# Four weight chunks of the fourth expert moved out of the ring, in a transformer block with 32 experts

## The chip, the cores and the metric

The kernel runs on one core of a Trainium2 chip. The metric is the device time of one execution in microseconds; the time before is the median of three runs. The profile is that of one execution. Its span runs from the first to the last instruction; its own device time, a little longer, stands beside it in the table below.

## The reference, cut to what matters

One layer over 512 tokens of width 2048, all in float32: a combined projection, sliding-window attention and trailing mean pools, an output projection, cross attention to 256 memory tokens, and then a mixture of experts:

```python
h = rmsnorm(x, ffn_norm_g)
g_sel  = argmax(h @ rg_w + rg_b)                    # one of 4 groups
top_v, top_i = top_k(e_logits of that group, 2)     # 2 of its 8 experts
y = (silu(xb @ w_gate[e]) * (xb @ w_up[e])) @ w_down[e]   # d_ff 512
x = x + sum over the 2 picks of gate * y
```

Each of the 32 experts has three float32 matrices of 2048 x 512 or 512 x 2048, 12 MiB together; all 32 are read, 384 MiB.

## The kernel before, in words

Front stages (attention, pools, output projection, cross attention) fill the first 700 us. The router follows: `turn_router` and `logits` on TensorE give the logits, a chain of small VectorE operations (L1299 to L1388) makes the tables of which token sits in which of the 64 slots of which expert, and GpSimd gathers the rows of the first two experts from `hn_dram`, a copy of the normed rows in device memory (`gather`, L588). Semaphore `logits_done` comes with the last logits, `table_ready` with the last table (L1388).

Then 32 expert blocks run, one for each expert, two to a pair. `block_pe(b, par, pair)` multiplies 64 slots with gate and up (L1893, 64 matmuls, chunks 0 to 7), then with down (L1921, 32 matmuls, chunks 8 to 11). In an even block it also adds the pair before to the tokens (`spread_parts`, L1870 with `y_hi` and L1871 with `y_lo`, the upper and lower half of the split rows; VectorE writes `y_lo` at L1423 and adds at L1405). At the end of the gate and up part of an odd block, `turn_rows` (L1850) turns the rows of the next pair, which the gather brought. Blocks 0 and 1 stand written out, blocks 2 to 31 are a loop over pairs.

The weights come through a ring of 12 buffers (`slot(s)`), one chunk of 1 MiB each, one expert in all. All weight loads are issued in order by SyncE (SP). `load_expert(e, b)` waits, before it loads chunk j, until TensorE has finished with chunk j of the block before (`used` counts finished chunks), and `landed[s]` tells TensorE of the arrival. The 12 chunks of expert 0 are issued while cross attention ends (L438), those of the others as blocks free their buffers (L444). `expert_slot(j)` gives the buffer of chunk j.

Buffers of SBUF are reused by hand. `Hf` is the buffer of transposed activations, of which the expert blocks use the first 3072 columns of 8192, and columns 4096 to 6143 under the name `y_lo` (tensor `below_y_low` is only there to place it). `PB` is the buffer of the projection: `hs[:, 0]` and `hs[:, 1]` are its first 4096 columns, the router's tables lie in 4096 to 8191, and the ramp of tokens in 6656 to 7167. `kx` and `vx` hold memory keys and values until cross attention ends; the router's padded logits `L` use part of `vx`.

Of the kernel before, what the change touches and what calls it, by code (L numbers as in the profile page):

```python
# [12 lines left out]
P = 128  # L13
F32 = mybir.dt.float32
I32 = mybir.dt.int32
F32R = mybir.dt.float32r
# [21 lines left out]
NE = NG * EPG  # L38
FF = 512
# [4 lines left out]
SLOTS = 64  # L44
# [8 lines left out]
POOL_BANKS = (4, 6, 7)  # L53
SCORE_BANKS = (0, 2, 1, 3)
NSLOT = 12
NA = 4
NCOL = NG + NE


def hybrid_block(nc, x, mem, mix_norm_g, w_in, q_norm_g, k_norm_g, sink_logits, pool_w, pool_scale,  # L60
# [5 lines left out]
    with ExitStack() as ctx:  # L66
        def sb(name, shape, dt=F32):
            return ctx.enter_context(nc.sbuf_tensor(name, shape, dt))

        def sem(name):  # L70
            return ctx.enter_context(nc.semaphore(name))
# [17 lines left out]
        X = sb("residual", [P, NT, D])  # L89
        with nc.sbuf_tensor("mix_high", [P, KD, S], F32R) as mix_hi:  # L90
            pass
        with ExitStack() as shared:
            shared.enter_context(nc.sbuf_tensor("below_y_low", [P, 4096], F32))
            y_lo = shared.enter_context(nc.sbuf_tensor("y_low", [P, 4, 512], F32R))
        H = sb("transposed_acts", [P, KD, S])
        with ExitStack() as shared:
            shared.enter_context(nc.sbuf_tensor("below_y", [P, 2 * D], F32))
# [4 lines left out]
        PB = sb("proj_buffer", [P, NCT * S])  # L102
        with ExitStack() as shared:
            tri_r = shared.enter_context(nc.sbuf_tensor("lower_triangle", [P, P], F32R))
            ones_r = shared.enter_context(nc.sbuf_tensor("ones_rounded", [P, P], F32R))
            M_r = shared.enter_context(nc.sbuf_tensor("picks_of_token", [P, NT + 1, NE], F32R))
            P_r = shared.enter_context(nc.sbuf_tensor("slot_of_pick", [P, 2 * NT, SLOTS], F32R))
            shared.enter_context(nc.sbuf_tensor("below_block_tokens", [P, 96], F32))
            Bv_r = shared.enter_context(nc.sbuf_tensor("block_tokens", [P, 2 * NT, TCOL], F32R))
        kx = sb("memory_keys_T", [P, XH, NM])  # L110
        vx = sb("memory_values", [P, NM // P, XW])
        ident = sb("identity", [P, P])
# [18 lines left out]
        def slot(s):  # L131
            return ring[:, s * CHK:(s + 1) * CHK]
# [20 lines left out]
        Hf = H[:, :, :].rearrange("p k s -> p (k s)")  # L153
        PTX = slot(7)[:, 0:1024]
        qn = slot(7)[:, 1024:1536].rearrange("p (h n) -> p h n", n=XD)
        junk = slot(7)[:, 1536:2048]
        xsT = Hf[:, 0:KD * P].rearrange("p (k n) -> p k n", n=P)
        act_t = Hf[:, 2048:2048 + KF * SLOTS]
        sil = Hf[:, 2304:2304 + KF * SLOTS]
        gu = Hf[:, 2560:2560 + FF]  # L160
# [27 lines left out]

        landed = [sem(f"landed{s}") for s in range(NSLOT)]
        used = sem("chunks_used")  # L190
        mem_in = [sem("mem_in0"), sem("mem_in1")]
        x_in = [sem(f"x_in{t}") for t in range(NT)]
        gain_in = sem("gain_in")
# [205 lines left out]
        def expert_chunk(e, j):  # L399

            if j < 8:
                return (gate_v, up_v)[j % 2][ds(e, 1), :, j // 2, :].rearrange("e p m -> p (e m)")
            return down_v[ds(e, 1), :, j - 8, :].rearrange("e p n -> p (e n)")


        def expert_slot(j):
            return (4, 5, 6, 0, 1, 2, 3, 7, 8, 9, 10, 11)[j]

        @block.sync
        def _(sp):  # L410
            for t in range(2):
                sp.dma_start(memx[:, t, :], mem[0, t * P:(t + 1) * P, :]).then_inc(mem_in[t], 16)
            for n, (s, src, width) in enumerate(early):
                if n in (2, 3):
                    for t in range(2 * n - 4, 2 * n - 2):
                        sp.dma_start(X[:, t, :], x[0, t * P:(t + 1) * P, :]).then_inc(x_in[t], 16)
                if n == SEQ_OUT + 1:
                    sp.wait_ge(halves_used, HALVES_IN)
                if n == SEQ_OUT + 3:
                    for t in range(NT):  # L420
                        sp.dma_start(X[:, t, :], x[0, t * P:(t + 1) * P, :]).then_inc(x_again, 16)
                if n == SEQ_XO:

                    sp.wait_ge(halves_used, HALVES_IN + 32)
                last = [m for m in range(n) if early[m][0] == s]
                if last:
                    sp.wait_ge(used, last[-1] + 1)
                sp.dma_start(slot(s).rearrange("p (k n) -> p k n", n=width), src).then_inc(landed[s], 16)
            for j in range(12):
                s = expert_slot(j)  # L430
                if 3 <= j < 6:
                    sp.wait_ge(used, SEQ_XQ + s + 1)
                if j == 6:
                    sp.wait_ge(xq_done, NT)
                if j == 7:
                    sp.wait_ge(o_done, 28)
                    sp.wait_ge(parts_done, 32)
                sp.dma_start(slot(s), expert_chunk(0, j)).then_inc(landed[s], 16)  # L438

            def load_expert(e, b):  # L440
                for j in range(12):
                    s = expert_slot(j)
                    sp.wait_ge(used, b * 12 + (UE - 12 + j + 1))
                    sp.dma_start(slot(s), expert_chunk(e, j)).then_inc(landed[s], 16)  # L444

            with sp.Fori(1, NE) as b:
                load_expert(b, b)
            sp.wait_ge(table_ready, 1)
            more = sp.value_load(meta[0:1, NOVER:NOVER + 1], min_val=0, max_val=NOVER)
            with sp.If(more > 0):  # L450
                with sp.Fori(0, NOVER) as j:
                    e = sp.value_load(meta[0:1, ds(j, 1)], min_val=0, max_val=NE - 1)
                    load_expert(e, j + NE)
            for t in range(NT):
                sp.wait_ge(sum_ready, 2 * t + 2)
                sp.dma_start(out[0, t * P:(t + 1) * P, :], X[:, t, :]).then_inc(stored, 16)
            sp.wait_ge(stored, 16 * NT)
# [993 lines left out]
        def _(pe):  # L1451
# [401 lines left out]

            def expert_landed(b, j):
                s = expert_slot(j)
                pe.wait_ge(landed[s], b * 16 + 16 * (early_loads[s] + 1))

            def spread_parts(before, half, last=False):

# [20 lines left out]
            def block_pe(b, par, pair):  # L1880
                if par == 0:
                    pe.wait_ge(xsT_ready, b * 2 + 4)
                wait_past(pe, gu_copied, b)
                for c in range(4):
                    for kk in range(4):
                        k = 4 * c + kk
                        for side in range(2):

                            j = 2 * c + side
                            if kk == 0:  # L1890
                                expert_landed(b, j)
                            w = slot(expert_slot(j)).rearrange("p (k n) -> p k n", n=FF)
                            ins = mm(ps[side * SLOTS:(side + 1) * SLOTS, 0, :], xsT[:, k, par * SLOTS:(par + 1) * SLOTS], w[:, kk, :],  # L1893
                                     start=(k == 0), stop=(k == KD - 1), skip_group_check=True)
                            if kk == 3:
                                ins.then_inc(used, 1)
                if par == 1:
                    if pair is not None:
                        pe.wait_ge(part_added, pair * 8)
                    turn_rows(1 if pair is None else pair + 1)  # L1900
                behind = par == 0 and pair is not None
                if behind:

                    pe.wait_ge(y_dve, b * 2)
                    pe.wait_ge(spread_ready, pair)
                    spread_parts(pair * 8 - 8, 0)
                pe.wait_ge(gu_copied, b + 1)
                for f in range(KF):
                    ins = turn(guT[:, f, :], gu[:, f * P:(f + 1) * P], ident[:, :])
                ins.then_inc(gu_turned, 1)  # L1910
                if behind:
                    spread_parts(pair * 8 - 8, 1)
                pe.wait_ge(act_ready, b + 1)
                wait_past(pe, y_dve, b * 2)
                for f in range(KF):
                    expert_landed(b, 8 + f)
                    w = slot(expert_slot(8 + f))
                    for n in range(4):

                        half = slice(n % 2 * SLOTS, (n % 2 + 1) * SLOTS)  # L1920
                        ins = mm(ps[half, 4 + n // 2, :], act_t[:, f * SLOTS:(f + 1) * SLOTS],  # L1921
                                 w[:, n * 512:(n + 1) * 512], start=(f == 0), stop=(f == KF - 1), skip_group_check=True)
                    ins.then_inc(used, 1)
# [1 line left out]
            turn_rows(0)  # L1925
            block_pe(0, 0, None)
            block_pe(1, 1, None)
            with pe.Fori(1, NE // 2) as it:
                b = it * 2
                block_pe(b, 0, it)  # L1930
                block_pe(b + 1, 1, it)
# [38 lines left out]
```

## Time and profile before

| | us |
|---|---|
| median of 3 runs | 1727.8 (1726.32 to 1733.53) |
| the profiled execution, device time | 1729.1 |
| its span | 1727.3 |
| TensorE busy | 1564.0 (91%) |
| VectorE busy | 613.5 (36%) |
| ScalarE busy | 334.6 (19%) |
| granted TensorE clock, mean | 0.984 of full speed |

Busy times overlap, and a share of the span is an average over stages with different limits. Times in the rows are counted from the span's start. PE is TensorE, PEld its weight load, DVE VectorE, ACT ScalarE, POOL GpSimd, SP SyncE. L12 is line 12 of the kernel before. A releaser (`<-`) is what ended an idle time.

### The profile page before, as it was taken

To read this page: it belongs to the slowest core of one execution; us is meant where nothing else is said; L and a number is where in the kernel's file an instruction comes from. 1 tells how busy PE (TensorE), PEld (TensorE's weight loads), DVE (VectorE), ACT (ScalarE), POOL (GpSimd) and SP (SyncE) were. 2 spreads that over 40 slices of the span, in tenths; PEclk is the share of its full clock that TensorE was granted. 3 is DMA by queue.
4 is the path that set the end of the run, shared out by engine and by line. 5 is a ranking of instruction groups with operands and counts; after the bars stand their busy time and mean duration, and the time that the engine had idled before them with its cause. 6 is when DMAs were issued, how large, how long until landed. Compare 5 with 4: busy or idle time off the path is not lost.

```text
span 1727.3 us, 18629 instructions
## 1 busy us (share of the span) xinstructions
PE 1564.0 (91%) x7036; PEld 862.8 (50%) x7036; DVE 613.5 (36%) x755; ACT 334.6 (19%) x600; POOL 152.4 (9%) x225
## 2 busy tenths in 40 slices
PE   6999999989999998789898899889889889889997
PEld 5587776768887446534343333333334333333433
DVE  3445656652224223423133232323313313232333
ACT  4222334342221234210101010010010101001010
POOL 1470045410000000000000000000000000000000
PEclk9999999999999999789999999999999999999999
DMA  7432322442216030479999999999999999999994
GB/s 269 122 92 79 89 59 73 143 133 98 98 49 268 1 122 34 161 291 421 421 422 421 422 421 422 421 422 422 422 422 422 422 421 421 421 422 421 421 420 188
DMA packets 114901, 484.36 MB, mean 280 GB/s; under 512 B 9410, under 2 KB 47404, under 8 KB 61868
## 3 DMA queue, kind: packets, MB, share of 16 engines
q1 hardware_dynamic: 110864, 470.84, 68.0%
q0 software_dynamic: 3264, 12.88, 2.0%
q8 instruction: 28, 0.46, 0.1%
q10 hardware_dynamic: 732, 0.07, 0.0%
q14 instruction: 13, 0.11, 0.0%
HBM read 484.81 MB, written 8.39 MB: 286 GB/s over the span
## 4 chain that ended last, share of the span: by engine, by line
PE 64%; DMA 22%; DVE 8%; ACT 3%; issue 2%; ACTq 0%; SPq 0%; DVEq 0%; POOLq 0%
DMA weight_ring<-in_expert_w_up_dram 21%; PE ps L1893 17%; PE ps L1645 10%; PE ps L1523 8%; PE ps L1921 7%; PE ps L1754 3%; PE ps L1870 3%; PE ps L1698 3%; DVE residual L1405 2%; PE ps L1871 2%; PE ps L1474 2%; PE ps L1485 2%; ACT weight_ring L739 1%; PE ps L1780 1%; DVE w_in_low L1009 1%
## 5 line engine op out<-in xcount | busy, mean ns | idle before, releaser
L1893 PE MATMUL ps<-weight_ring,transposed_acts 128*64 128x512 f32 x2048 | 468.9, 595 | 66.6 <-DMA weight_ring<-in_expert_w_up_dram 65.9
L1893 PEld LDWEIGHTS ps<-weight_ring,transposed_acts 128*64 128x64 f32 x2048 | 153.0, 137 | 376.7 <-issue 252.9
L1405 DVE TENSOR_TENSOR residual<-ps,residual 128x1024 f32<-128x1024 f32 x128 | 151.4, 1221 | 261.5 <-PE ps L1871 260.1
L1921 PE MATMUL ps<-weight_ring,transposed_acts 128*64 128x512 f32 x1024 | 226.8, 595 | 19.1 <-DVE transposed_acts L1412 19.1
L1423 DVE SCALAR_TENSOR_TENSOR y_low<-ps,proj_buffer,y_high 64x1024 fp32r<-64x1024 f32 x64 | 82.1, 1283 | 211.3 <-ACT y_high L910 210.3
L1921 PEld LDWEIGHTS ps<-weight_ring,transposed_acts 128*64 128x64 f32 x1024 | 71.8, 137 | 155.5 <-issue 152.6
L910 ACT ACTIVATE y_high<-ps,proj_buffer 64x1024 fp32r<-64x1024 f32 x64 | 71.0, 1110 | 306.3 <-PE ps L1921 305.5
L1870 PE MATMUL ps<-y_high,spread 128*128 128x512 f32 x256 | 113.9, 445 | 14.2 <-DVE residual L1405 10.0
L1523 PE MATMUL ps<-mix_high,w_in_high 128*128 128x512 f32 x288 | 116.7, 405 | 1.3 <-issue 1.3
L1523 PE MATMUL ps<-normed_low,w_in_high 128*128 128x512 f32 x288 | 112.3, 390 | 0.0
L1523 PE MATMUL ps<-mix_high,w_in_low 128*128 128x512 f32 x288 | 112.3, 390 | 0.0
L902 ACT ACTIVATE transposed_acts<-ps 128x512 f32<-128x512 f32 x32 | 19.2, 599 | 475.6 <-PE ps L1893 475.6
L1871 PE MATMUL ps<-y_low,spread 128*128 128x512 f32 x256 | 102.6, 401 | 0.0
L1645 PE MATMUL ps<-weight_high,mix_high 128*128 128x512 f32 x256 | 99.8, 390 | 0.0
L1645 PE MATMUL ps<-weight_low,mix_high 128*128 128x512 f32 x256 | 99.6, 389 | 0.0
L1412 DVE TENSOR_TENSOR transposed_acts<-transposed_acts,ps 128x256 f32<-128x256 f32 x32 | 13.3, 417 | 216.9 <-ACT transposed_acts L905 216.9
L1009 DVE TENSOR_TENSOR w_in_low<-weight_ring,w_in_high 128x1024 fp32r<-128x1024 f32 x36 | 47.6, 1326 | 100.7 <-ACT w_in_high L695 100.6
L1870 PEld LDWEIGHTS ps<-y_high,spread 128*128 128x128 f32 x256 | 48.9, 191 | 66.1 <-DVE residual L1405 42.4
L585 POOL CAST slot_columns<-proj_buffer 128x1 int32 (+1 forms) x16 | 3.0, 186 | 868.8 <-PE ps L1850 868.8
L1143 DVE TENSOR_TENSOR weight_low<-weight_ring,weight_high 128x1024 fp32r<-128x1024 f32 x32 | 38.6, 1226 | 69.7 <-ACT weight_high L789 69.7
L1523 PEld LDWEIGHTS ps<-mix_high,w_in_high 128*128 128x128 f32 x288 | 54.1, 188 | 15.9 <-issue 4.3
L1523 PEld LDWEIGHTS ps<-normed_low,w_in_high 128*128 128x128 f32 x288 | 54.1, 188 | 13.0 <-issue 2.2
(261 smaller groups left out, 1681.8 us busy)
## 6 DMA issues: line engine op xcount, KB each, us to landing
weight_ring<-in_expert_w_gate_dram SPq DMA_DIRECT2D x128, 1024.0 KB, 24.0
weight_ring<-in_expert_w_up_dram SPq DMA_DIRECT2D x128, 1024.0 KB, 25.9
weight_ring<-in_expert_w_down_dram SPq DMA_DIRECT2D x128, 1024.0 KB, 19.0
weight_ring<-in_w_in_dram SPq DMA_DIRECT2D x18, 1024.0 KB, 5.6
weight_ring<-in_w_out_dram SPq DMA_DIRECT2D x16, 1024.0 KB, 5.0
weight_ring<-in_xkv_w_dram SPq DMA_DIRECT2D x8, 1024.0 KB, 6.6
residual<-in_x_dram SPq DMA_DIRECT2D x8, 1024.0 KB, 16.3
weight_ring<-in_xq_w_dram SPq DMA_DIRECT2D x4, 1024.0 KB, 9.5
```

What stands on the lines that cost most here:

```text
L910: a.activation(y_hi[par * SLOTS:(par + 1) * SLOTS, side:4:2, :], ps[rows, 4:6, :], ACT.Copy, scale=gate[rows, ds(b, 1)]).then_inc(y_act, 1)
L1009: v.tensor_tensor(in_lo[:, half], raw, in_hi[:, half].bitcast(F32), ALU.subtract).then_inc(w_lo_ready, 1)
L1405: v.tensor_tensor(part, ps[:, bank:bank + 2, :].rearrange("p b n -> p (b n)"), part, ALU.add).then_inc(sum_ready if last else part_added, 1)
L1423: v.scalar_tensor_tensor(out=y_lo[par * SLOTS:(par + 1) * SLOTS, side:4:2, :], in0=ps[rows, 4:6, :], scalar=gate[rows, ds(b, 1)], in1=y_hi ...
L1523: ins = mm(ps[:, bank, :].rearrange("p (t n) -> p t n", n=P), w_[:, half, kk, :], h_, start=(k == 0 and part == 0), stop=(k == KD - 1 and ...
L1645: ins = mm(ps[:, 4 * (n % 2) + t, :], m_, w_[:, r, kk, :], start=(u % 8 == 0 and kk == 0 and part == 0), stop=(u % 8 == 7 and kk == 1 and ...
L1698: ins = mm(ps[:, 4 + t % 2, :], H[:, k, t * P:(t + 1) * P], w[:, kk, :], start=(k == 0), stop=(k == KD - 1))
L1754: ins = mm(ps[:, n % 2, :], H[:, c, t * P:(t + 1) * P], chunk(SEQ_XO + c, D)[:, 0, n * 512:(n + 1) * 512], start=(c == 0), stop=(c == 3))
L1870: mm(ps[:, bank, :], spread[:, t * P:(t + 1) * P], y_hi[:, cols_, :], start=True, stop=False)
L1871: ins = mm(ps[:, bank, :], spread[:, t * P:(t + 1) * P], y_lo[:, cols_, :], start=False, stop=True)
L1893: ins = mm(ps[side * SLOTS:(side + 1) * SLOTS, 0, :], xsT[:, k, par * SLOTS:(par + 1) * SLOTS], w[:, kk, :], start=(k == 0), stop=(k == KD ...
L1921: ins = mm(ps[half, 4 + n // 2, :], act_t[:, f * SLOTS:(f + 1) * SLOTS], w[:, n * 512:(n + 1) * 512], start=(f == 0), stop=(f == KF - 1), ...
```

## The change

Expert 3 (`EXTRA`) gets its chunks 0 to 3 from buffers outside the ring: `hs[:, 1]`, two pieces of `Hf`, and for chunk 3 two half pieces (1024 columns each), one at the end of `Hf`'s free part and one where router tables lay. SP issues these five loads between expert 0's and expert 1's, each behind a wait. Expert 3 then loads 8 chunks through the ring, and expert 4's first four chunks take buffers that block 2 has freed (`behind=2`). TensorE takes the weights of block 3 from `expert_weights`, with blocks 2 and 3 written out ahead of the loop, and `landed` counts one less for those four buffers. `y_lo` moves from `Hf` to where `kx` and part of `vx` are.

```diff
+EXTRA = 3
-        with ExitStack() as shared:
-            shared.enter_context(nc.sbuf_tensor("below_y_low", [P, 4096], F32))
-            y_lo = shared.enter_context(nc.sbuf_tensor("y_low", [P, 4, 512], F32R))
+        with nc.sbuf_tensor("y_low", [P, 4, 512], F32R) as y_lo:
+            pass
         kx = sb("memory_keys_T", [P, XH, NM])
+        extra = [[PB[:, 2048:4096]], [Hf[:, 4096:6144]], [Hf[:, 6144:8192]], [Hf[:, 3072:4096], PB[:, 7168:8192]]]
+            def load_extra(j):
+                at = 0
+                for buf in extra[j]:
+                    n = buf.shape[1]
+                    sp.dma_start(buf, expert_chunk(EXTRA, j)[:, at:at + n]).then_inc(extra_in, 16)
+                    at += n
+            sp.wait_ge(hn_stored[1], 32)
+            sp.wait_ge(h_turned, 56)
+            load_extra(0)
+            sp.wait_ge(logits_done, 1)
+            load_extra(1)
+            load_extra(2)
+            sp.wait_ge(table_ready, 1)
+            load_extra(3)
-            def load_expert(e, b):
-                for j in range(12):
+            def load_expert(e, b, first=0, behind=1):
+                for j in range(first, 12):
                     s = expert_slot(j)
-                    sp.wait_ge(used, b * 12 + (UE - 12 + j + 1))
+                    back = behind if j < 4 else 1
+                    sp.wait_ge(used, (b - back + 1) * 12 + (UE - 12 + j + 1))
                     sp.dma_start(slot(s), expert_chunk(e, j)).then_inc(landed[s], 16)
-            with sp.Fori(1, NE) as b:
+            for b in range(1, EXTRA):
                 load_expert(b, b)
-            sp.wait_ge(table_ready, 1)
+            load_expert(EXTRA, EXTRA, first=4)
+            load_expert(EXTRA + 1, EXTRA + 1, behind=2)
+            with sp.Fori(EXTRA + 2, NE) as b:
+                load_expert(b, b)
...
             def expert_landed(b, j):
                 s = expert_slot(j)
-                pe.wait_ge(landed[s], b * 16 + 16 * (early_loads[s] + 1))
+                if isinstance(b, int) and b == EXTRA and j < 4:
+                    pe.wait_ge(extra_in, 16 * 5)
+                else:
+                    left_out = 1 if j < 4 and not (isinstance(b, int) and b < EXTRA) else 0
+                    pe.wait_ge(landed[s], b * 16 + 16 * (early_loads[s] + 1 - left_out))
+            def expert_weights(b, j, kk):
+                if isinstance(b, int) and b == EXTRA and j < 4:
+                    parts = extra[j]
+                    each = 4 // len(parts)
+                    return parts[kk // each].rearrange("p (k n) -> p k n", n=FF)[:, kk % each, :]
+                return slot(expert_slot(j)).rearrange("p (k n) -> p k n", n=FF)[:, kk, :]
...
             block_pe(1, 1, None)
-            with pe.Fori(1, NE // 2) as it:
+            block_pe(2, 0, 1)
+            block_pe(3, 1, 1)
+            with pe.Fori(2, NE // 2) as it:
```

## Rows read from the trace of the kernel before

**Rows 1.** The page: granted clock in tenths and GB/s, 40 slices of 43.2 us

```profile
PEclk9999999999999999789999999999999999999999
GB/s 269 122 92 79 89 59 73 143 133 98 98 49 268 1 122 34 161 291 421 421 422 421 422 421 422 421 422 422 422 422 422 422 421 421 421 422 421 421 420 188
```

**Rows 2.** Stretches: length, busy (instructions) of PE, PEld, DVE, ACT, POOL, clock, DMA share, GB/s

```profile
712.00:720.00 8.00, 8.00 (x40) 8.00 (x38) 2.00 (x3) 0.00 (x0) 0.68 (x2) 0.50 0.98 374
720.00:723.00 3.00, 0.27 (x2) 0.13 (x1) 2.45 (x8) 0.00 (x0) 0.00 (x0) 0.50 0.88 371
723.00:734.00 11.00, 2.24 (x13) 2.07 (x13) 8.92 (x35) 0.31 (x2) 0.00 (x0) 0.50 0.00 0
740.00:746.00 6.00, 5.20 (x24) 3.90 (x26) 2.77 (x4) 0.00 (x0) 1.22 (x2) 0.72 0.00 0
750.00:762.00 12.00, 9.72 (x48) 3.34 (x46) 0.42 (x1) 2.27 (x3) 0.00 (x0) 1.00 1.00 423
911.00:972.00 61.00, 54.84 (x252) 22.05 (x250) 18.00 (x20) 6.40 (x8) 1.19 (x2) 1.00 1.01 422
```

**Rows 3.** The chain that ended last, expert stage: start, length, what

```profile
837.73 25.33 DMA weight_ring<-in_expert_w_up_dram
898.07 26.02 DMA weight_ring<-in_expert_w_up_dram
959.11 26.02 DMA weight_ring<-in_expert_w_up_dram
...
1636.35 24.68 DMA weight_ring<-in_expert_w_up_dram
```

**Rows 4.** Waits of PE, 847 to 1661 us: total, times, longest

```profile
PE ps L1893 <- DMA weight_ring<-in_expert_w_up_dram: 64.5, 53, 1.6
```

**Rows 5.** PE in order of time: start, length, line [idle before]

```profile
744.36 13.95 PE L1893 MATMUL ps<-weight_ring,transposed_acts 128*64 128x512 f32 x64 [0.78 <-DVE transposed_acts L1394]
792.25 14.17 PE L1893 MATMUL ps<-weight_ring,transposed_acts 128*64 128x512 f32 x64
847.41 4.46 PE L1893 MATMUL ps<-weight_ring,transposed_acts 128*64 128x512 f32 x18
```

**Rows 6.** SP in order of time: loads issued

```profile
705.65 2.16 SPq L438 DMA_DIRECT2D weight_ring<-in_expert_w_down_dram  x4
748.21 0.35 SPq L444 DMA_DIRECT2D weight_ring<-in_expert_w_gate_dram  x1
...
818.22 5.62 SPq L444 DMA_DIRECT2D weight_ring<-in_expert_w_down_dram  x4
```

**Rows 7.** The chain that ended last, router stage

```profile
734.72 5.25 DMA proj_buffer<-normed_rows,slot_columns
740.01 3.58 PE ps L1850 x16
```

**Rows 8.** Router stage in order of time: store of rows, last table, second gather

```profile
710.16 0.53 POOL L564 DMA_DIRECT2D normed_rows<-proj_buffer  x1 [20.68 <-ACT proj_buffer L858]
737.79 0.20 DVE L1388 COPY proj_buffer<-ps 64x50 f32<-64x50 f32 x1
744.69 1.03 POOL L588 DMA_INDIRECT proj_buffer<-normed_rows,slot_columns  x1 [0.85 <-POOL slot_columns L585]
```

**Rows 9.** Time to landing: that store; the 16 gathers after 744 us

```profile
DMA to landing us min/median/max: 10.6/10.6/10.6
DMA to landing us min/median/max: 4.2/8.8/10.0
```

**Rows 10.** The end of the kernel, PE in order of time

```profile
1709.95 0.80 PE L1870 MATMUL ps<-y_high,spread 128*128 128x512 f32 x1 [4.05 <-DVE y_low L1423]
1710.55 0.63 PE L1871 MATMUL ps<-y_low,spread 128*128 128x512 f32 x1
...
1716.09 0.41 PE L1870 MATMUL ps<-y_high,spread 128*128 128x512 f32 x1
```

More of the change, by code:

```diff
@@ L190, in hybrid_block @@
         used = sem("chunks_used")
+        extra_in = sem("extra_in")
         mem_in = [sem("mem_in0"), sem("mem_in1")]
@@ L1891, in block_pe @@
                                 expert_landed(b, j)
-                            w = slot(expert_slot(j)).rearrange("p (k n) -> p k n", n=FF)
-                            ins = mm(ps[side * SLOTS:(side + 1) * SLOTS, 0, :], xsT[:, k, par * SLOTS:(par + 1) * SLOTS], w[:, kk, :],
+                            ins = mm(ps[side * SLOTS:(side + 1) * SLOTS, 0, :], xsT[:, k, par * SLOTS:(par + 1) * SLOTS], expert_weights(b, j, kk),
                                      start=(k == 0), stop=(k == KD - 1), skip_group_check=True)
```

## The prediction, made before the changed kernel ran

> **What bounds the kernel now.** I read the page's slices first. From slice 19 on (777 us), GB/s stands at 421 or 422 in every slice to the last but one [rows 1]. A rate that never moves, whatever the compute beside it does, is the mark of a queue that is never empty. The stretches make it sharper: 423 GB/s at a DMA share of 1.00 already in 750 to 762 us, 422 at 1.01 later, and 0 GB/s in 723 to 734 and in 740 to 746 [rows 2]. So there is a full stage after 750 us and idle time ahead of it.
>
> Next the chain of waits. In the expert stage its long pieces are loads of expert_w_up: one starts at 837.73 and takes 25.33 us, the next start at 898.07 and 959.11 and take 26.02, the last starts at 1636.35 and takes 24.68 [rows 3]. The reader should not take 25 us for the price of a load; it is the time in a queue with some ten loads ahead. Start and length give the ends, 863.06, 924.09, 985.13, and so the pace: 61.03 us for a pair of experts. TensorE loses 64.5 us in 53 waits for these loads from 847 to 1661 us, 1.6 at the most each [rows 4]: it is close behind the stream everywhere. Before that it does not wait: the pair of blocks 2 and 3 runs from 792.25 to 847.41, 55.16 us [rows 5]. A pair costs TensorE 55.2 us when nothing is late, and the stream 61.0.
>
> So the end of the kernel is set by one stream: it starts at 748.21, when the first chunk of expert 0 has been used [rows 6], reaches full rate by 750, and carries 31 x 12 = 372 chunks. After the wait that ends at 1661.02 comes a fixed tail of 66.3 us.
>
> **The change part by part.**
>
> *The chunks taken out of the stream.* Expert 3 brings 8 chunks instead of 12, so 368 remain. A pair moves 61.0 us x 422 GB/s = 25.74 MB [rows 2]: 24 chunks of 1.0486 MB and 0.57 MB of gathered rows. One chunk is 1.0486/422 = 2.485 us, and four are 9.94 us. This is the term of the sum.
>
> *Where they go.* Five loads (three of 1 MiB, two of half) are issued ahead of expert 1's. SP has nothing between its last load of expert 0, out by 707.8, and 748.21 [rows 6], so nothing is queued behind the new waits but those loads. Extra 0 waits for the last store of rows: issued 710.16, landing 10.6 us later, 720.8 [rows 8, 9]. Extras 1 and 2 wait for the logits, done by then. The queues are busy with expert 0's rest and that store to about 722.9 (374 and 371 GB/s, then none) [rows 2]; three chunks end at 722.9 + 7.5 = 730.4, inside the stretch that moved nothing. The gather of the first pair starts at 734.72 [rows 7], 4.3 us later. Extra 3 waits for the last table, 737.79 + 0.20 = 738.0 [rows 8]. From issue to full rate it took 748.21 to 750, 1.8 us; so its data runs from 739.8 to 742.3, while the gather lands at 739.97 [rows 7] and the second is issued at 744.69 [rows 8]. All four hide in idle time: cost 0. If that cover fails, the bounds are these. Below, nothing can be gained here: the only transfer on the chain in this stage is the gather. Above, a gather between full queues takes 8.8 us (median of 16) against 5.25 [rows 9, 7], so block 0 and the stream that follows it start 3.6 us later. I take 0, as the nearest row is the empty stretch.
>
> *Whether the shorter stream stays full.* The risk is that the stream, four chunks ahead, catches up with TensorE freeing buffers. Old chunk 44 (expert 4's last gate or up chunk) landed at 863.06. Expert 3's chunk 7 becomes the 28th: 863.06 less 16 x 2.485, less about 0.7 to 1.3 for a gather between, is 822.0 to 822.6. The next load needs the first down buffer that block 2 frees; it is issued at 818.22, the four within 5.62 us [rows 6]. Issue plus 1.8 is 820.0: about 2 us in hand, and 1.8 us between frees against 2.485 for a load, so the margin grows. Expert 4's first four chunks need only buffers freed by block 2's gate and up, and follow at once; its fifth and sixth need block 3, which frees them around 833.8, with the stream busy until 841.9. Cost 0, at the top 1 us, if the 16 engines don't end together. Below 0 is excluded: a full stream can't be fuller.
>
> *When the gain reaches the end.* TensorE starts block 0 at 744.36 as before and, never late, starts pairs at 847.41, 902.6 and 957.7. It wants the last up chunk 10.3 us after each (three of four 3.43 us parts): 857.7, 912.9, 968.0. The stream lands them at 853.1, 914.1, 975.2 (old times less 9.94). So it waits not at all in block 4, 1.2 us in block 6, 7.2 in block 8, and from there it is the old state, 9.94 us earlier. Its spare time of 5.9 us a pair makes the switch in two pairs out of fourteen.
>
> *Blocks 2 and 3 written out, and SP's experts 1 to 4.* The same matmuls; two waits take constants. On entering the loop's next pair at 847.41 the row has no idle time before it [rows 5], so there is no price of a branch to save. Cost 0, and up to block 8 a few tenths would be absorbed.
>
> *The low half of the split rows moved.* Writers (L1423) and readers (L1871) keep number and shape. Its memory was the keys', dead since cross attention, and the padded logits, read last long before the first write after block 0. Cost 0. If each of L1871's matmuls took 0.05 us more, that is 0.8 us a pair, less than the 5.9 spare: only the last pair's 0.8 would show; as much less is the other bound.
>
> *The end.* The last pair's sums start at half clock, 0.43 us from one matmul to the next [rows 10] where later ones take 0.23. About 14 of them cost 2.8 us. All this moves 9.94 us earlier with the same idle stretch before it (4.05 us) [rows 10], so I take no change, with 2.8 us as bound in both directions.
>
> **The sum.** The profiled execution took 1729.1 us (span 1727.3). 1729.1 - 9.94 = 1719.2. The median of the runs, 1727.8, is 1.3 lower, so the forecast is **1717.9 us**, 0.58% less.
>
> **The rivals.**
>
> 1. *The cover leaks.* The gather of the first pair meets extra 3, or the stream runs dry before the down chunks. For it: extra 3's data begin when the gather ends, to a few tenths. Against: 2 us in hand at block 2. Price 1.5 to 4.6 us, so 1719.4 to 1722.5: within 0.5%.
> 2. *TensorE becomes the bound.* If a pair cost TensorE as much as the stream, being early would bring nothing: 1727.8. Against: 55.16 against 61.03 [rows 5, 3], and the clock is granted in full (9 is 90% or more) from slice 19 on [rows 1].
> 3. *The gather queues behind the extras: slower.* The mechanism is at the first gather alone. It sets block 0, block 0's first freed buffer sets the stream, so each microsecond it is late is one at the end. It decides in favour of slower when the delay passes 9.94 us, that is, if more than four chunks are still unserved at 734.7. The rows price the worst: a load with some ten ahead takes 26 us [rows 3] against 5.25, a delay of 20.8, and 1727.8 - 9.9 + 20.8 = 1738.7. Against: 11 us with no byte moved, of which three chunks need 7.5; and gathers land after 8.8 us where loads take 25 [rows 9, 3], so a gather does not stand behind all of them. The Trainium skill ("DMA: Bandwidth & Descriptors", Queues, rings and completion order) says that each DMA engine takes turns between the queue rows it has work for, a packet at a time; by that rule the delay is a sharing and not the whole queue, and the gathers' 8.8 us agree.
> 4. *The end's half clock goes as well.* Then 2.8 us more: 1715.1. For it: the stretch at half clock ends at 1716 for no reason in the kernel's order [rows 10]. Against: the same idle time comes before it.
> 5. *A chunk is worth more.* If loads ran at the 374 GB/s of 712 to 720 us [rows 2], a chunk would take 2.80 us and four 11.2: 1716.6. Against: 422 and 423 wherever only weights and gathers move [rows 2]. The Trainium skill ("DMA: Bandwidth & Descriptors", Specifications) gives about 358 GB/s as a core's limit from device memory; by that rule four chunks would be 11.7 us and the kernel 1716.1. This trace, with one core running, disagrees with 422, and the measurement decides.
>
> **How the numbers follow.** What this kernel's measurement can tell from no change is about 0.5%, 8.6 us; faster means under 1719.2. Forecast 64%, rival 1 22%, rival 2 4%, rival 3 3%, rival 4 5%, rival 5 2%. Forecast and rivals 4 and 5 make 0.71; the forecast lies only 1.3 us inside the bound, so 0.05 of it goes to within: faster 0.66. Within 0.5% are rivals 1 and 2 and those 0.05, 0.31; slower is rival 3, rounded up with 0.01 from these for what I have not thought of: 0.30 and 0.04. The range goes from 1714.5 (rival 4 and half a microsecond) to 1722.5 (rival 1's top).
>
> **What would show it.** Right: five loads between 720 and 740 us, GB/s above 0 in 723 to 734; the gather still 5.3 us; TensorE's first L1893 at 744.4; SP's first ring load at 748.2; no DMA wait in block 4, a full wait in block 8; 422 GB/s without a gap from 750; last wait's end near 1651. Wrong: block 0 later than 745, a stretch between 815 and 835 under 415 GB/s, pairs above 61 us with TensorE not waiting, or a tail other than 66 us.

## The result, and the profile after

The changed kernel took 1719.6 us (median of 7 runs, 1717.86 to 1720.96) beside 1727.8 for the kernel before (7 runs, 1722.29 to 1733.69): ratio 0.9943, interval 0.9923 to 0.9962. In a second series, on the same chip as four other kernels, it was 0.9936, 0.9917 to 0.9956 (6 runs, median 1717.05). The forecast was 1717.9 us and 9.9 us of gain; the two series measured 8.2 and 10.6. The profiled execution took 1719.06 us, its span is 1717.3, 10.0 less than before.

The slices of the page, granted clock and GB/s, answer to [rows 1]:

```profile
PEclk9999999999999999789999999999999999999999
GB/s 271 123 87 85 79 69 74 124 153 97 92 57 252 18 123 25 235 284 422 419 421 422 422 422 422 421 421 422 421 422 421 422 421 421 422 421 420 420 421 189
```

The plateau is the same. Slice 17 rose from 161 to 235 GB/s: 3 MB came forward into it. The stretches of [rows 2] (length, busy of PE, PEld, DVE, ACT and POOL, clock, DMA share, GB/s):

```profile
720.00:723.00 3.00, 0.77 (x4) 0.80 (x4) 2.73 (x12) 0.30 (x2) 0.00 (x0) 0.50 1.02 399
723.00:734.00 11.00, 3.13 (x27) 2.92 (x26) 8.96 (x32) 0.01 (x1) 1.09 (x1) 0.50 0.74 288
740.00:746.00 6.00, 5.22 (x16) 2.09 (x16) 1.65 (x3) 0.00 (x0) 1.21 (x2) 0.50 0.27 83
750.00:762.00 12.00, 9.72 (x48) 3.28 (x46) 0.42 (x1) 2.26 (x3) 0.00 (x0) 1.00 1.01 427
812.00:820.00 8.00, 7.72 (x34) 3.47 (x34) 5.16 (x6) 0.00 (x0) 0.00 (x0) 1.00 1.00 415
820.00:835.00 15.00, 15.00 (x74) 5.04 (x72) 2.56 (x2) 2.23 (x2) 0.00 (x0) 1.00 1.02 421
911.00:972.00 61.00, 54.90 (x251) 22.26 (x249) 18.04 (x19) 6.40 (x8) 1.18 (x2) 1.00 1.01 421
```

The 11 us that moved nothing now carry 288 GB/s. The narrow place at 812 to 835 us, where the stream could have caught up with the buffers, shows 415 and then 421: the 415 is worth 0.1 us. SP's queue in order of time, the answer to [rows 6]:

```profile
721.03 0.33 SPq L446 DMA_DIRECT2D proj_buffer<-in_expert_w_gate_dram  x1
721.41 0.42 SPq L446 DMA_DIRECT2D transposed_acts<-in_expert_w_up_dram  x1
721.88 0.43 SPq L446 DMA_DIRECT2D transposed_acts<-in_expert_w_gate_dram  x1
734.87 0.33 SPq L446 DMA_DIRECT2D transposed_acts<-in_expert_w_up_dram  x1
735.24 1.29 SPq L446 DMA_DIRECT2D proj_buffer<-in_expert_w_up_dram  x1
748.04 0.33 SPq L463 DMA_DIRECT2D weight_ring<-in_expert_w_gate_dram  x1
```

The five loads came out ahead of the ring's first, which stands at 748.04 where it stood at 748.21. TensorE in the blocks that make the switch (start, length, idle before):

```profile
846.99 13.90 PE L1925 MATMUL ps<-weight_ring,transposed_acts 128*64 128x512 f32 x64
...
901.89 11.32 PE L1925 MATMUL ps<-weight_ring,transposed_acts 128*64 128x512 f32 x50
914.45 3.65 PE L1925 MATMUL ps<-weight_ring,transposed_acts 128*64 128x512 f32 x14 [1.23 <-DMA weight_ring<-in_expert_w_up_dram]
...
965.57 3.65 PE L1925 MATMUL ps<-weight_ring,transposed_acts 128*64 128x512 f32 x16 [1.32 <-DMA weight_ring<-in_expert_w_up_dram]
```

Block 4's gate and up part is done in one piece, block 6 (901.89) waits once, 1.23 us, for its last up chunk, and block 8 waits four times (0.46, 1.32, 1.32 and 1.31 us), once for each up chunk, as the blocks did before. That is the hand-over from TensorE's own pace to the stream's. The chain's weight loads, the first two and the last, against [rows 3]:

```profile
892.21 22.20 DMA weight_ring<-in_expert_w_up_dram
949.42 26.03 DMA weight_ring<-in_expert_w_up_dram
...
1626.42 24.76 DMA weight_ring<-in_expert_w_up_dram
```

They end at 914.41, 975.45 and 1651.18, where the old ones ended at 924.09, 985.13 and 1661.02: 9.7, 9.7 and 9.8 us earlier. The tail behind the last is 66.1 us after 66.3.

### The profile page after: what moved, and what is told of

Read it like the earlier page. It is cut to its first block, busy times and chain, and to the rows that moved or that the text cites. A ratio compares the mean times of both kernels' runs of the same rounds, so it can differ in the third digit from the quotient of the medians.

```text
span 1717.3 us, 18475 instructions
## 1 busy us (share of the span) xinstructions
PE 1560.7 (91%) x7036; PEld 859.3 (50%) x7036; DVE 612.9 (36%) x755; ACT 334.5 (19%) x600; POOL 152.2 (9%) x225
## 4 chain that ended last, share of the span: by engine, by line
PE 66%; DMA 20%; DVE 8%; ACT 3%; issue 2%; ACTq 0%; SPq 0%; DVEq 0%; POOLq 0%
DMA weight_ring<-in_expert_w_up_dram 20%; PE ps L1925 18%; PE ps L1667 10%; PE ps L1545 8%; PE ps L1953 8%; PE ps L1776 3%; PE ps L1903 3%; PE ps L1720 3%; DVE residual L1427 3%; PE ps L1904 2%; PE ps L1496 2%; PE ps L1507 2%; ACT weight_ring L761 1%; DVE w_in_low L1031 1%; PE ps L1802 1%
## 5 line engine op out<-in xcount | busy, mean ns | idle before, releaser
L1925 PE MATMUL ps<-weight_ring,transposed_acts 128*64 128x512 f32 x2016 | 462.0, 597 | 59.4 <-DMA weight_ring<-in_expert_w_up_dram 58.6
L1953 PE MATMUL ps<-weight_ring,transposed_acts 128*64 128x512 f32 x1024 | 226.8, 595 | 18.9 <-DVE transposed_acts L1434 18.9
L1903 PEld LDWEIGHTS ps<-y_high,spread 128*128 128x128 f32 x256 | 48.8, 191 | 66.1 <-DVE residual L1427 42.3
```

What stands on the lines that cost most here:

```text
L1903: mm(ps[:, bank, :], spread[:, t * P:(t + 1) * P], y_hi[:, cols_, :], start=True, stop=False)
```

## The experiments

All theories speak of one stream, so one quantity is read from every profile: the span less the time at which SP issues the ring's first load. It leaves out everything that happens in the router. There is one profile of each, so the rows with the same count show how far the difference can be trusted: 979.1 and 979.8 for 372 chunks, 969.3 to 970.0 for 368, 963.7 to 965.0 for 366.

| kernel | chunks in the stream | first ring load | span | difference |
|---|---|---|---|---|
| before | 372 | 748.21 | 1727.3 | 979.1 |
| changed | 368 | 748.04 | 1717.3 | 969.3 |
| changed, again | 368 | 750.94 | 1720.3 | 969.4 |
| three chunks | 369 | 746.57 | 1717.5 | 970.9 |
| no extra | 372 | 746.93 | 1726.7 | 979.8 |
| for expert 1 | 368 | 752.30 | 1722.3 | 970.0 |
| beside the gather | 368 | 754.94 | 1724.3 | 969.4 |
| for expert 2 | 368 | 748.17 | 1718.1 | 969.9 |
| expert 3 left out | 360 | 747.60 | 1711.0 | 963.4 |
| six outside | 366 | 750.81 | 1715.2 | 964.4 |
| six, again | 366 | 747.05 | 1710.7 | 963.7 |
| six, kept busy | 366 | 744.04 | 1709.0 | 965.0 |

**Three chunks.** `NX` is the number of chunks held outside.

```diff
+NX = 3
...
-            sp.wait_ge(table_ready, 1)
-            load_extra(3)
...
-            load_expert(EXTRA, EXTRA, first=4)
+            load_expert(EXTRA, EXTRA, first=NX)
```

> Of the changed kernel, chunk 3 goes back into the ring: three extra loads, expert 3 brings 9 chunks by the ring. My theory (the loads from 750 us on are one full stream, and a chunk taken out of it is worth 2.485 us): 3 x 2.485 = 7.5 us less than before, 1720.3 with before at 1727.8, and 2.5 us over the changed kernel; the chain's last weight wait ends about 2.5 us later than in the changed kernel (1651.2 there). Rival (the cover leaks: chunk 3's two half loads meet the first gather and cost part of what they save): this kernel comes within 1 us of the changed one.

1721.17 us, ratio 0.9941, 0.992 to 0.9961: 7.9 us under before, 7.5 expected. The difference in the table, 970.9, lies 8.2 under before and 1.6 over the changed kernel. The times alone don't tell three chunks from four. The table leans to the count (971.8 by 2.485 us a chunk), with 0.9 to 1.6 us over the five rows with 368 chunks; this run alone does not exclude the rival. The chain's last weight wait ended at 1651.9, not at 1653.7: this run's first ring load came 1.5 us earlier, which the expectation had left out.

**No extra.** The same with `NX = 0` and without the extra loads: what is left of the change is the other place of `y_lo` and the code written out.

> The low half of the split rows stays where the change puts it, and blocks 2 and 3 and SP's loads of experts 1 to 4 stay written out, but no load is taken out of the ring. My theory: these two edits cost and bring nothing, within 1 us of before. Rival (they gave or took part of the difference: the code written out stalls TensorE, or its two weight streams read faster or slower from the new place): more than 2 us away from before on either side, and the pair of blocks 2 and 3 not 55.2 us.

1729.43 us beside 1729.07, ratio 0.9994, 0.9979 to 1.001. The pair of blocks 2 and 3 ran from 791.14 to 846.23, 55.1 us. The interval still allows 3.6 us of gain, and the table (979.8 against 979.1) shows none: no worth of these two edits is seen, and the gain is in the loads.

**For expert 1.**

```diff
-EXTRA = 3
+EXTRA = 1
```

> EXTRA = 1: the same five loads at the same time and the same 368 chunks in the stream, but they are expert 1's first four. The ring's first load is then expert 1's chunk 4, whose buffer block 0 frees at 754.9 and not at 748.0. My theory (what counts is when the stream starts, how many chunks it has, and that it is never empty): it starts 6.9 us later, so of 9.9 us only 3.1 are left: 1724.7 with before at 1727.8, 6.9 over the changed kernel. Rival (the gain is that TensorE finds four chunks early, whichever they are): as the changed kernel, within 1 us of it.

1726.49 us, 0.9989, 0.9976 to 1.0002: 2.6 us of gain, 3.1 expected. The five loads are the same and as early as in the changed kernel, and TensorE has its four chunks; the gain is gone because the stream starts later:

```profile
752.30 0.33 SPq L463 DMA_DIRECT2D weight_ring<-in_expert_w_gate_dram  x1
```

Here block 0 started at 741.75, and SP could issue the load at 752.30, 10.55 us later, where the changed kernel's needed only block 0's first chunk. From there on it is the same (970.0). So the rival, that chunks held early are what counts, falls.

**Beside the gather.**

```diff
+            sp.wait_ge(first_ids, 2)
             load_extra(0)
```

> The first three extra loads also wait for the token numbers of the first pair, so that they are issued together with the first gather instead of 11 us ahead of it. My theory (the gather sets block 0, block 0's first freed buffer sets the stream, and that the end): the gather lands later than the 5.3 to 6.0 us of the two profiles, and every microsecond it is late is one at the end. The price from the saturated gathers (8.8 us): 2.8 to 3.6 us over the changed kernel, 1723 with before at 1727.8. Rival 3 of the prediction (the gather stands behind all loads issued before it): three chunks and more, 7.5 us. Other rival (the stream's start does not depend on it): as the changed kernel.

1725.84 us, 0.9973, 0.9957 to 0.9989: 3.2 us under before where the changed kernel has 8.2 or 10.6, so it costs some 5 to 7 us where 2.8 to 3.6 were expected. The two half loads of extra 3 kept their wait and were issued 3.3 us after the gather. The gather and what follows, from the chain, from the issues (KB, median us to landing) and from TensorE in order of time:

```profile
734.88 10.00 DMA proj_buffer<-normed_rows,slot_columns
```

```profile
transposed_acts<-in_expert_w_gate_dram SPq DMA_DIRECT2D x1, 1024.0 KB, 10.0
proj_buffer<-normed_rows,slot_columns POOLq DMA_INDIRECT x1, 10.0
```

```profile
744.92 3.68 PE L1873 MATMUL ps<-identity,proj_buffer 128*128 128x128 f32 x16 [7.33 <-DMA proj_buffer<-normed_rows,slot_columns]
749.38 15.83 PE L1926 MATMUL ps<-weight_ring,transposed_acts 128*64 128x512 f32 x64 [0.78 <-DVE transposed_acts L1417]
```

The gather took 10.00 us, not 8.8, against 5.25 before [rows 7]: 4.75 more. And block 0 began on the half clock, so that the first ring load came 5.56 us after its start, not 3.85 as before (744.36 to 748.21). Together 6.5 us, and 754.94 less 748.21 is 6.7. My price was a gather's time among a full queue, without the clock. The half clock is not a cost of this edit: block 0 began on it in five other profiles too, two of them of the unedited changed kernel. Against the changed kernel's second profile, whose clock fell alike, the first ring load is 4.0 us later. The theory's main point holds: behind the first load the difference is 969.4 again, so each microsecond there went to the end.

The second fence has the last of the three loads of 1 MiB and the gather: both were issued at 734.88 and landed after 10.0 us. The first two loads had landed at 738.7 and 743.6; the half loads landed at 746.2 and 748.6. So here the gather came no earlier than any of the three, which is rival 3's mechanism. Its price of 7.5 us was too high, as part of the waiting falls into the 5.25 us that a gather takes anyway. The Trainium skill ("DMA: Bandwidth & Descriptors", Queues, rings and completion order) says each DMA engine takes turns between queue rows. The gather moves some 0.4 MB (72 GB/s in 734 to 740 us of the trace before), about 1 us at 422 GB/s, so an even sharing would add an estimated 1 us; 4.75 is far above that, while in the full stream gathers landed after 8.8 us where loads took 25 [rows 9, 3], far from standing behind all. What order holds in general stays open.

**The changed kernel again.** No edit.

> The changed kernel once more, beside the before kernel on the same chip. My theory: span less first ring load is 969.2 (969.3 in its first profile, 979.1 before), whatever the router's clock does; the times differ by 9.9 us, and what is off that in the medians (8.2 so far) is scatter of the time of the first ring load, 746.5 to 748.2 in profiles so far. Rival (some of the 9.9 us is given back behind the first ring load): the difference stays at 8 and span less first load lies above 970.5.

1717.05 us beside 1727.68: 10.6 less, and 969.4 behind a first ring load at 750.94, later than the 746.5 to 748.2 expected. The rival that part is given back falls. Over both series the 13 runs of the changed kernel have their median at 1718.3.

**Expert 3's other chunks left out.**

```diff
-            load_expert(EXTRA, EXTRA, first=4)
...
-                    left_out = 1 if j < 4 and not (isinstance(b, int) and b < EXTRA) else 0
+                    left_out = 0 if isinstance(b, int) and b < EXTRA else 1
```

> None of expert 3's last 8 chunks is loaded (block 3 multiplies what is left in the ring), so 360 chunks are in the stream, 8 fewer than in the changed kernel. Rival (every chunk out of the stream is worth 2.485 us): 19.9 us less than the changed kernel, 1699.7. My theory (only while the stream is never empty): after expert 4's first four chunks, done at about 822, the next buffer comes free with block 3's fourth and fifth chunk, 833.4, so the DMA engines are idle for some 13 us between 822 and 835, and of 19.9 us 6.7 are left: 1713 with the changed kernel at 1719.6.

1711.12 us (4 runs), 5.9 under the changed kernel of the same series; 6.7 expected by my theory, 19.9 by the rival. The stretches show the hole:

```profile
812.00:818.00 6.00, 5.73 (x24) 2.75 (x26) 4.74 (x5) 0.00 (x0) 0.00 (x0) 1.00 1.02 423
818.00:822.00 4.00, 4.00 (x20) 1.29 (x18) 0.00 (x0) 0.00 (x0) 0.00 (x0) 1.00 0.50 209
822.00:826.00 4.00, 4.00 (x22) 1.38 (x20) 1.89 (x2) 2.22 (x2) 0.00 (x0) 1.00 0.02 4
826.00:830.00 4.00, 4.00 (x22) 1.34 (x20) 0.67 (x1) 0.00 (x0) 0.00 (x0) 1.00 0.00 0
830.00:834.00 4.00, 4.00 (x20) 1.29 (x18) 0.00 (x0) 0.00 (x0) 0.00 (x0) 1.00 0.07 10
834.00:838.00 4.00, 4.00 (x27) 2.27 (x24) 0.00 (x0) 0.60 (x1) 0.00 (x0) 1.00 0.93 356
```

From 820 to some 834 us almost nothing moves while TensorE is fully busy: the next buffer is not free. Eight chunks left out are 19.9 us, the hole takes about 14 back. A stream bound by the DMA engines is bound by buffers as soon as it gets far enough ahead.

**For expert 2.** `EXTRA = 2`.

> EXTRA = 2: the same loads and the same 368 chunks, but expert 2's first four. The stream has loaded expert 1 by 781.1, and expert 2's chunk 4 needs the buffer that block 1 frees at 778.7, with data from 780.5: no gap or one under a microsecond. My theory: as the changed kernel, or up to 1.3 us over it. Rival (the lead of four chunks must be taken late, by expert 3): 3 us and more over it, as with expert 1.

1717.35 us (4 runs) beside 1717.05: the same, with 969.9 in the table, 0.6 over. So expert 2 serves as well as expert 3, and expert 1 is too early.

**Six outside.** Two more chunks, expert 1's first two in `early_two`, and SP's order changed so that neither the start nor the narrow place suffers:

```diff
+        early_two = [[PB[:, 4096:6144]], [kx[:, :, :].rearrange("p h n -> p (h n)"), vx[:, :, :].rearrange("p m n -> p (m n)")]]
...
             load_extra(3)
+            for j in range(2):
+                for n, buf in enumerate(early_two[j]):
+                    w = buf.shape[1]
+                    sp.dma_start(buf, expert_chunk(1, j)[:, n * w:(n + 1) * w]).then_inc(two_in, 16)
...
-            for b in range(1, EXTRA):
-                load_expert(b, b)
-            load_expert(EXTRA, EXTRA, first=4)
-            load_expert(EXTRA + 1, EXTRA + 1, behind=2)
+            load_expert(2, 2, behind=2, last=2)
+            load_expert(1, 1, first=2)
+            load_expert(2, 2, first=2)
+            load_expert(3, 3, first=4, last=8)
+            load_expert(4, 4, behind=2, last=4)
+            load_expert(3, 3, first=8)
+            load_expert(4, 4, first=4)
...
-                act.wait_ge(used, b * 12 + (UE + 12))
+                act.wait_ge(used, b * 12 + (UE + 12) + (2 if isinstance(b, int) and b == 0 else 0))
```

> Two more chunks outside the ring: expert 1's chunks 0 and 1, in the buffers of the split rows (where the router tables and the memory keys were), loaded right behind extra 3 in the 7 us that the changed kernel leaves idle before its first ring load. ScalarE's first y_high write waits until block 1 has used them (about 771.8 where it was 768.4; read only after 792). SP issues expert 2's first two chunks first, and expert 4's first four ahead of expert 3's down chunks, so that the stream doesn't run dry. My theory: 366 chunks in the stream, span less first ring load 964.3, 4.97 us less than the changed kernel, 14.9 less than before: 1714.6 at before's 1727.8. Rivals: the added loads delay block 0 or the second gather (first ring load later than 748.5), or the stream runs dry at 806 to 820 us (a stretch under 410 GB/s): then 1 to 4 us less than the changed kernel, or nothing.

> The kernel with six chunks outside once more, beside the one above. Span less first ring load 964.4; 14.9 us less than before by my theory. Rival (part of two chunks is given back): 11 to 13 less.

1711.85 us beside 1727.68, 0.9904, 0.9883 to 0.9925; and 1713.65 beside 1727.65, 0.9927, 0.9904 to 0.995. That is 15.8 and 14.0 us under before, 14.9 expected. The differences are 964.4 and 963.7. In the profiles the first ring load came at 750.81 and 747.05. The first lies beyond the 748.5 set as the sign of a delay, but the changed kernel without the two chunks had 750.94, so it shows none. The idle time before the ring and the narrow place are full in the first profile:

```profile
740.00:748.00 8.00, 6.96 (x24) 4.28 (x26) 2.77 (x4) 0.00 (x0) 1.22 (x2) 0.50 1.01 402
...
805.00:815.00 10.00, 9.60 (x44) 4.97 (x40) 4.76 (x5) 0.98 (x2) 0.00 (x0) 1.00 1.02 424
815.00:825.00 10.00, 9.72 (x43) 4.23 (x44) 4.90 (x5) 0.00 (x0) 0.00 (x0) 1.00 1.02 422
```

In the series that they share it is 5.2 us under the changed kernel (1711.85 and 1717.05); the intervals of their ratios to before (0.9883 to 0.9925, 0.9917 to 0.9956) overlap by a little, and the table's 4.9 us (964.4 against 969.3) is the firmer number; over all its rows of 368 and 366 chunks without the added matmuls it is 4.9 to 6.3.

**Six, and TensorE kept busy.**

```diff
+            def keep_busy(n):
+                for _ in range(n):
+                    mm(ps[:, 6, :], ident[:, :], X[:, 0, 0:512], start=True, stop=True)
...
+            keep_busy(5)
```

`keep_busy(5)` stands behind the logits; 6, 2 and 2 follow behind the three groups of table products.

> The kernel with six chunks outside, and 15 matmuls of 512 columns whose result nobody reads, in TensorE's four idle stretches of the router stage (720 to 740 us, 5.1, 5.7, 2.2 and 2.6 us long). They test where the scatter of the first ring load comes from (746.6 to 750.9 us in eight profiles with the same work before it). My theory (TensorE's granted clock in the router stage and in block 0's first matmuls): the clock is back at full speed by 740, the turns of L1872 take about 2.1 us and not 3.7, block 0's first four products 3.4 and not 5.8; the first ring load comes at 743.5 to 747, and the time goes down by 1 to 5 us against the kernel without them; span less first load stays 964.4. Rival (the scatter is in the gather or the DMA engines): no change of the first load. Other rival (the added matmuls overrun and delay the chain): first load later by up to 1 us.

1711.41 us beside 1713.65 of the kernel without them in the same series; ratios to before 0.9906 (0.9883 to 0.9929) and 0.9927 (0.9904 to 0.995) overlap, so a gain of 2.2 us is not shown. The profiles show where a gain would come from, first without them (the same kernel, six again), then with:

```profile
739.17 3.38 PE L1881 MATMUL ps<-identity,proj_buffer 128*128 128x128 f32 x16 [2.93 <-DMA proj_buffer<-normed_rows,slot_columns]
743.37 13.95 PE L1942 MATMUL ps<-weight_ring,transposed_acts 128*64 128x512 f32 x64 [0.82 <-DVE transposed_acts L1425]
```

```profile
737.03 1.97 PE L1889 MATMUL ps<-identity,proj_buffer 128*128 128x128 f32 x16 [0.54 <-DMA proj_buffer<-normed_rows,slot_columns]
740.36 13.96 PE L1950 MATMUL ps<-weight_ring,transposed_acts 128*64 128x512 f32 x64 [1.36 <-DVE transposed_acts L1425]
```

The turns take 1.97 us instead of 3.38, and block 0 starts 3.0 us earlier; the gather, 4.31 us instead of 5.61, and its issue, 0.85 us earlier, make up the rest, less 0.54 us of a longer gap before block 0. Block 0's gate and up part is the same, 13.96 and 13.95, as the clock was back in time in both. In executions in which it was not, block 0 pays too, as in the changed kernel's second profile:

```profile
744.83 16.38 PE L1925 MATMUL ps<-weight_ring,transposed_acts 128*64 128x512 f32 x64 [0.78 <-DVE transposed_acts L1416]
```

That is 2.4 us more, all in its first products. Whether the added matmuls prevent this for good, one profile cannot show. The first ring load came at 744.04, the earliest of all profiles. The difference behind it is 965.0, 0.6 to 1.3 over the other two with six chunks; why is open.

## Why the prediction was right

*The stream as the bound.* In eleven of twelve profiles the span is the first ring load plus a constant for the count of chunks, to 1.3 us; the twelfth is the one whose stream runs dry. Between 372 and 368 chunks of the profiled pair lie 9.8 us, 2.46 a chunk where 2.485 was worked out; over all rows with these counts it is 9.1 to 10.5 us. "No extra" shows no other part of the change at work.

*The start of the stream: right by luck.* The forecast took the router for fixed: block 0 at 744.4, first ring load at 748.2. The first ring load did come at 748.04, but by two differences that cancel. The 32 products of `logits(3)` took 4.12 us where they had taken 6.88, and for the most part this put the gather's issue 3.14 us earlier; block 0 began at 742.03. Then block 0 began on the half clock, and its first buffer came free 6.01 us after its start and not 3.85. Neither comes from the change: the changed kernel's second profile has the 6.88 us and the slow block 0, and its first ring load at 750.94. So the profiled pair's 10.0 us is as near to 9.94 as it is by chance; the 9.8 us behind the first ring load is the part that the working had right.

*The cover.* Three chunks were in flight from 721 on, at 434 GB/s to 730.4 us and 116 from there to the gather's issue. The issue, at 731.58, came 1.2 us after that and not the 4.3 us reckoned with, again through the faster logits. The gather took 5.96 us in the changed kernel's first profile and 5.57 in the second, against 5.25 before. That is no cost of the extra loads: with no extra load at all ("No extra") it took 5.70, and with three chunks and nothing beside it 5.00. The cost of 0 stands; the upper bound was too low: with three loads issued together with the gather it is 4.75 us and not 3.6.

*The full stream.* It stayed full (415 and 421 GB/s), but with less in hand than the 2 us reckoned. With expert 3's other chunks left out, the 28th load of the stream was done at 820.0, 72.4 us after the first ring load. The same 72.4 us from 748.04 give 820.4 for the changed kernel. Its first down buffer came free at 817.96 and, with 1.8 us from issue to full rate, was in use at 819.8: an estimated 0.6 us in hand.

*The hand-over.* No wait in block 4, 1.23 us in block 6 (1.2 forecast), the old state from block 8. The 7.2 us forecast for block 8 count block 6's wait a second time; without it they are 6.0. The four waits shown there come to 4.4.

*The rivals.* TensorE as the bound: 58.6 us of waits remain of 64.5 [rows 4]. In the pairs of blocks 4 and 6 they fell by 3.9 and 3.2 us, as the hand-over wants, and over the rest they rose by 1.2. The gather behind the extras is real as a mechanism, and where it was made to happen the kernel was still 3 us faster than before: not enough to turn the sign. The end's half clock stayed: the last sums again start 0.43 us apart. A chunk worth more, at 374 GB/s, would be 11.2 us for four; the rows give 10.5 at the most.

*The size.* The profiled pair differs by 10.0 us, the medians by 8.2 and 10.6. The scatter of single runs, 1721.8 to 1734.1 for before, is larger than the error of the sum. Profiles place it ahead of the stream: first ring loads between 746.57 and 750.94 us for kernels with the same TensorE work ahead of it.

## What to carry to other kernels

When one rate stands flat over a whole stage, the stage is worth bytes over that rate, and a byte moved into idle time ahead of it is gained one to one, as long as the stream neither starts later for it nor runs dry. So two places set the limit: when the stream's first transfer can be issued, and the first place where it catches up with the buffers; both can be worked out in advance from the issue times of the profile, and the order of issue can be changed to widen them. Read a common mark (here the span less the first ring load) from each profile: for equal counts of chunks it agreed here to 0.7 us (1.3 with the added matmuls), so that differences of 2.5 us and more are told apart, where single runs of one kernel lie up to 12 us apart.

## What the runs showed of the hardware

A gather issued together with three loads of 1 MiB landed after 10.00 us, with the last of them. In the other eleven profiles the first gather took 4.31 to 5.96 us; the 5.25 before and the 5.70 of "No extra" had no weight load beside them, so the differences within this band can't be put down to the loads.

TensorE's clock in the router and in block 0 shifts the start of the weight stream of the following 950 us. In the same order of work, `logits(3)`, 32 small products, took 6.88 us in the trace before and 4.12 in that of the changed kernel (granted clock 0.50, the level of 1.2 GHz, all through 712 to 720 us, and 0.71 on the average, with TensorE busy all 8 us of the former). The clock came back to 2.4 GHz before block 0 in six profiles, whose gate and up part took 13.95 to 13.96 us, and only after its first products in the other six, with 15.8 to 16.5 us. The first ring load followed block 0's start by 3.7 to 6.2 us. The fast `logits(3)` did not go with a fast block 0: of the four profiles with 4.1 us, three had the slow one. What sets the moment stays open. With the idle stretches filled with unread matmuls the clock was 0.89 in 720 to 726 us and 1.00 from 726 on, against 0.50 in 720 to 740 us without them.
